# Prompt row sums of a product-key expert layer divided between TensorE and VectorE, with gelu values stored by token tile

## The chip, the cores and the metric

The kernel runs on one core of one Trainium2 chip. The metric is the device time of one execution in microseconds (us). Before the change three runs took 2674.08, 2677.42 and 2680.5 us; their median is 2677.42 us.

## The reference, cut to what matters

A two-layer trunk handles 384 tokens of width 1024: 128 prompt tokens (token tile 0) and 256 latent tokens (tiles 1 and 2). Each layer mixes the tokens (retention and mLSTM in layer 0, attention in layer 1) and then runs `_peer`, the part that is changed here. For each token and each of 8 heads, `_peer` picks 16 of 16384 experts, so 128 experts per token, with a softmax gate:

```
act = gelu(einsum("thkd,td->thk", u_tab[ib], xb)) * gb
out = einsum("thk,thkd->td", act, v_tab[ib])
```

`u_tab` and `v_tab` have 16384 rows of 1024 fp32 values (64 MB each per layer).

## The kernel before, in words

`peer_front` and `peer_experts` work through the 16384 experts as 128 **blocks** of 128. In the hidden stage (blocks 0 to 63 in `peer_front`, 64 to 127 in `peer_experts`), TensorE computes gelu inputs of one block for all 384 tokens; ScalarE applies gelu into `hidden_ring`, and the result goes to the DRAM tensor `hidden`. For the latent tokens VectorE multiplies the values of every expert by a gate (zero where an expert was not picked).

The **output stage** follows. Latent tokens are computed densely: for each of 128 blocks, `outs` makes 12 matmuls of 128x512 for the two latent tiles from `v_hi`, `v_lo` (the block of `peer_v` split into two fp32r parts) and `act_hi`, `act_lo` (the gated gelu values, split likewise). For each block ScalarE makes `v_hi` (L2164), and VectorE makes `v_lo` (L2300), `act_hi` (L2309) and `act_lo` (L2310). These parts have three buffers, so the parts of block o wait for TensorE to end block o-3. SyncE loads 2 MB of `peer_v` and 512 KB of gated values (`hidden_in`) for each four blocks, into two buffers each.

The 128 prompt tokens are not computed densely. Their 128 picked rows of `peer_v` are fetched by indirect DMA: one **row** DMA (L2212) brings the 128 rows of one token, 4 KB to each of 128 partitions, into one of `RING` = 11 slots. A **pick** DMA (L2220) brings the 128 gelu values of one token. Four tokens make one quad, 32 quads in all. `act_columns` (L2319, VectorE) multiplies the quad's gelu values by its gates into columns that are zero elsewhere, and `row_sums` (L2105, TensorE) multiplies those columns with the rows: eight 128x512 products per quad, which the profile shows as 16 instructions. `SET_AFTER` puts a set of two quads behind block 15 and every seventh block after that, 16 sets in all.

All engines work in program order. The places where they wait for each other in this stage:
- TensorE waits in `row_sums` for the columns (`acts_made`) and for the rows (`slot_in`).
- GpSimd issues row and pick DMAs in one fixed sequence. `row(j)` with j >= RING waits until the quad that used the slot is summed (`rows_summed`); everything behind it in the sequence waits too. The sequence starts when the last hidden values are in DRAM (`hg_out`), apart from `FREE` = 2 rows that are fetched earlier.
- VectorE waits for ScalarE's `v_hi`, for `hidden_in`, and in `act_columns` for the pick DMAs.

Behind the last block VectorE normalises tile 0 (whose sum is complete first), then tiles 1 and 2 (`norm_half`, L876 to L889), and writes the result.

## Time and profile before

| what | value |
|---|---|
| median of 3 runs | 2677.42 us |
| profiled execution: its own time | 2680.38 us |
| profiled execution: span | 2678.6 us |
| TensorE (PE) busy | 2604.6 us, 97% of the span |
| VectorE (DVE) busy | 1658.9 us, 62% |
| ScalarE (ACT) busy | 1022.3 us, 38% |
| GpSimd (POOL) busy | 720.7 us, 27% |
| output stage, layer 0, of which GpSimd issues | 990 to 1356 us |
| output stage, layer 1: first block to last row sums | 2256.44 to 2646.07 us |

The span runs from the first to the last instruction on the core; the profiled execution's own time is 1.8 us longer. Busy shares are averages over stages with different limits. Row sums, pick DMAs and row DMAs exist only in the two output stages, one per layer.

### The profile page before, as it was taken

To read this page: it belongs to the slowest core of one execution; us is meant where nothing else is said; L and a number is where in the kernel's file an instruction comes from. 1 tells how busy PE (TensorE), PEld (TensorE's weight loads), DVE (VectorE), ACT (ScalarE), POOL (GpSimd) and SP (SyncE) were. 2 spreads that over 40 slices of the span, in tenths; PEclk is the share of its full clock that TensorE was granted. 3 is DMA by queue.
4 is the path that set the end of the run, shared out by engine and by line. 5 is a ranking of instruction groups with operands and counts; after the bars stand their busy time and mean duration, and the time that the engine had idled before them with its cause. 6 is when DMAs were issued, how large, how long until landed. Compare 5 with 4: busy or idle time off the path is not lost. (4 is left out here: it accounts for less than half of the span.)

```text
span 2678.6 us, 39466 instructions
## 1 busy us (share of the span) xinstructions
PE 2604.6 (97%) x15833; PEld 2307.6 (86%) x15833; DVE 1658.9 (62%) x3306; ACT 1022.3 (38%) x1531; POOL 720.7 (27%) x688
## 2 busy tenths in 40 slices
PE   7998999999999999999999889999999999999998
PEld 6997789999999997777779679999999999777775
DVE  3447687879344456555576569987934445655556
ACT  3444433345433333333352554334543333333333
POOL 1001020000111117777723003000011111777773
PEclk9998899999999999999999989999999999999999
DMA  9653486547798869999964124344779886999995
GB/s 307 219 170 139 148 300 215 165 189 287 262 360 317 315 217 388 391 383 382 386 254 127 64 97 137 119 147 188 287 266 365 313 312 217 391 389 390 393 385 202
DMA packets 233941, 708.88 MB, mean 265 GB/s; under 512 B 22432, under 2 KB 154912, under 8 KB 211488
## 3 DMA queue, kind: packets, MB, share of 16 engines
q1 hardware_dynamic: 172912, 516.86, 52.7%
q0 software_dynamic: 60032, 189.01, 19.2%
q8 instruction: 127, 2.08, 0.3%
q10 hardware_dynamic: 816, 0.48, 0.1%
q14 instruction: 54, 0.44, 0.0%
HBM read 602.31 MB, written 103.98 MB: 264 GB/s over the span
## 5 line engine op out<-in xcount | busy, mean ns | idle before, releaser
L1410 PE MATMUL hidden_ps<-h_hi,u_hi 128*128 128x384 f32 x2016 | 680.3, 337 | 4.1 <-issue 3.1
L1410 PE MATMUL hidden_ps<-h_hi,u_lo 128*128 128x384 f32 x2016 | 674.0, 334 | 0.0
L1410 PE MATMUL hidden_ps<-h_lo,u_hi 128*128 128x384 f32 x2016 | 674.0, 334 | 0.0
L2300 DVE TENSOR_TENSOR v_lo<-v_slot,v_hi 128x1024 fp32r<-128x1024 f32 x248 | 303.9, 1225 | 269.2 <-ACT v_hi L2164 269.2
L2164 ACT ACTIVATE v_hi<-v_slot 128x1024 fp32r<-128x1024 f32 x248 | 263.0, 1060 | 515.0 <-PE out_ps L2093 503.0
L2093 PE MATMUL out_ps<-v_hi,act_hi 128*128 128x512 f32 x992 | 389.7, 393 | 0.0
L2093 PE MATMUL out_ps<-v_lo,act_hi 128*128 128x512 f32 x992 | 386.3, 389 | 0.0
L2093 PE MATMUL out_ps<-v_hi,act_lo 128*128 128x512 f32 x992 | 385.9, 389 | 0.0
L1410 PEld LDWEIGHTS hidden_ps<-h_hi,u_hi 128*128 128x128 f32 x2016 | 378.6, 188 | 6.9 <-issue 6.8
L1410 PEld LDWEIGHTS hidden_ps<-h_lo,u_hi 128*128 128x128 f32 x2016 | 378.7, 188 | 0.0
L1410 PEld LDWEIGHTS hidden_ps<-h_hi,u_lo 128*128 128x128 f32 x2016 | 378.5, 188 | 0.0
L2282 DVE TENSOR_TENSOR u_lo<-u_slot,u_hi 128x1024 fp32r<-128x1024 f32 x124 | 151.9, 1225 | 289.0 <-ACT u_hi L2149 289.0
L2220 POOL DMA_INDIRECT first_act<-hidden,hidden_number x256 | 272.9, 1066 | 154.1 <-issue 77.4
L2212 POOL DMA_INDIRECT row_slot<-in_peer_v,row_number x256 | 262.9, 1027 | 123.9 <-issue 67.7
L2093 PEld LDWEIGHTS out_ps<-v_hi,act_hi 128*128 128x128 f32 x992 | 186.1, 188 | 65.1 <-DVE act_lo L2310 16.4
L1764 DVE TENSOR_TENSOR u_lo<-u_slot,u_hi 128x1024 fp32r<-128x1024 f32 x132 | 164.2, 1244 | 119.2 <-ACT u_hi L1685 116.3
L2093 PEld LDWEIGHTS out_ps<-v_hi,act_lo 128*128 128x128 f32 x992 | 186.2, 188 | 39.0
L2093 PEld LDWEIGHTS out_ps<-v_lo,act_hi 128*128 128x128 f32 x992 | 186.2, 188 | 37.4
L1692 ACT ACTIVATE hidden_ring<-hidden_ps 128x384 f32<-128x384 f32 x128 | 63.0, 492 | 357.9 <-PE hidden_ps L1410 353.0
L2156 ACT ACTIVATE hidden_ring<-hidden_ps 128x384 f32<-128x384 f32 x128 | 63.0, 492 | 347.5 <-PE hidden_ps L1410 341.4
L2229 POOL MEMSET act_columns<- 128x1008 f32 x2 | 1.9, 945 | 569.5 <-POOLq L1422 569.5
L1685 ACT ACTIVATE u_hi<-u_slot 128x1024 fp32r<-128x1024 f32 x128 | 134.7, 1053 | 0.0
(502 smaller groups left out, 3968.9 us busy)
## 6 DMA issues: line engine op xcount, KB each, us to landing
u_slot<-in_peer_u SPq DMA_DIRECT2D x64, 2048.0 KB, 9.1
v_slot<-in_peer_v SPq DMA_DIRECT2D x64, 2048.0 KB, 9.9
hidden<-hidden_ring SPq DMA_DIRECT2D x64, 768.0 KB, 5.8
spread_gates<-spread SPq DMA_DIRECT2D x16, 2048.0 KB, 7.2
hidden_in<-hidden SPq DMA_DIRECT2D x64, 512.0 KB
ada_w_ring<-in_ada_w SPq DMA_DIRECT2D x48, 512.0 KB, 6.1
even_w_ring<-in_even_w SPq DMA_DIRECT2D x16, 1024.0 KB, 7.5
ada_w_ring<-in_ada_w SPq DMA_DIRECT2D x16, 1024.0 KB, 6.1
```

The lines of the kernel that those rows point to most:

```text
L1410: mm = pe.matmul(PH_[:, b, 0:T], u[:, b, k * P:(k + 1) * P], x[:, k, :], start=(k == 0 and part == 0), stop=(k == KB - 1 and part == 2))
L1685: act.activation(UH[:, n % 2, :], U[n // JC % 2][:, n % JC, :], ACT.Copy).then_inc(uh, 1)
L1692: act.activation(HG[:, m % 2, j, :], PH_[:, n % 2, 0:T], ACT.Gelu_apprx_tanh).then_inc(g_done, 1)
L1764: dve.tensor_tensor(UL[:, n % 2, :], U[n // JC % 2][:, n % JC, :], UH[:, n % 2, :].bitcast(F32), ALU.subtract).then_inc(ul, 1)
L2093: mm = pe.matmul(PO[:, t, c, :], a[:, at], x[:, c * CH:(c + 1) * CH], start=(o == 0 and part == 0), stop=(o == N_KEYS - 1 and part == 2), ...
L2156: act.activation(HG[:, m % 2, j, :], PH_[:, n % 2, 0:T], ACT.Gelu_apprx_tanh).then_inc(g_done, 1)
L2164: act.activation(hi, V[o // JC % 2][:, o % JC, :], ACT.Copy).then_inc(vh, 1)
L2212: pool.indirect_dma_start(ROWS[j % RING], None, table, bass.IndirectOffsetOnAxis(ap=IDXV[:, t:t + 1], axis=0)).then_inc(slot_in[j % RING], 16)
L2220: pool.indirect_dma_start(ACT0[:, t:t + 1], None, hidden, bass.IndirectOffsetOnAxis(ap=IDXG[:, t:t + 1], axis=0)).then_inc(pick_in[i % 8], 16)
L2229: pool.memset(SDW, 0.0).then_inc(zeroed, 1)
L2282: dve.tensor_tensor(UL[:, n % 2, :], U[n // JC % 2][:, n % JC, :], UH[:, n % 2, :].bitcast(F32), ALU.subtract).then_inc(ul, 1)
L2300: dve.tensor_tensor(lo, V[o // JC % 2][:, o % JC, :], hi.bitcast(F32), ALU.subtract).then_inc(vl, 1)
```

## The change

The prompt's 128 picks per token are halved. `HALF_PICKS` = 64.

- **TensorE's half.** One row DMA now brings 64 picks of two tokens (partitions 0 to 63 and 64 to 127), so that 64 row DMAs and 16 quads cover the 128 tokens. Each of the 16 places in `SET_AFTER` has one quad instead of two. The ring for these rows (`RING`) has 5 slots.
- **VectorE's half.** The other 64 picks of each token are fetched by 64 DMAs (`own_row`) that bring one picked row for each of the 128 tokens, a token to a partition. VectorE adds each to `row_sum`, weighted by a number per partition (`add_own_row`, one instruction of 128x1024). Four of them stand around each set, behind blocks -1, 0, +2 and +3 of it (`OWN_AFTER`). Their ring `OWN` has 6 slots, taken from the old ring of 11. At the end `row_sum` is added to tile 0's sum in PSUM, by two instructions of 128x512.
- **GpSimd's sequence** is rewritten: eight pick DMAs per quad instead of four, and the own rows between them. The count of indirect DMAs per layer stays at 256 (64 rows, 64 own rows, 128 picks).
- **act_hi** is made by ScalarE (`act_high`) instead of VectorE, ahead of `v_hi` of the same block.
- **gelu values by tile.** `hidden` and `hidden_ring` are laid out tile by tile, so that the two latent tiles of four blocks are 4 KB in one piece per partition instead of four pieces of 1 KB. VectorE's gating takes two instructions of half the size.
- In the front, the picks of tile 0 are transposed in paired form: one more VectorE copy, six more small ScalarE instructions, four more small VectorE instructions for the indices, once per layer.

```diff
-                RING, FREE = len(SLOT_AT), 2
+                RING, FREE = 5, 2
...
+                OWN = ROWS[RING:]
+                SUM0 = M.at("row_sum", 4096, [P, D])
...
-                QUADS = P // 4
-                SET = 2
-                SET_AFTER = [15 + 7 * i for i in range(16)]
+                QUADS = HALF_PICKS // 4
+                SET_AFTER = [15 + 7 * i for i in range(QUADS)]
+                OWN_AFTER = {SET_AFTER[j // 4] + (-1, 0, 2, 3)[j % 4]: j for j in range(HALF_PICKS)}
...
-                        sp.dma_start(HV[:, c % 2], HD[:, c, :, P:T]).then_inc(hg_in[c % 2], 16)
+                        sp.dma_start(HV[:, c % 2], HD[:, c, 1:TT]).then_inc(hg_in[c % 2], 16)
...
+                    def own_row(j):
+                        n, at = j % len(OWN), HALF_PICKS + j
+                        if j >= len(OWN):
+                            pool.wait_ge(own_added, j - len(OWN) + 1)
+                        pool.indirect_dma_start(OWN[n], None, table,
+                                                bass.IndirectOffsetOnAxis(ap=IDXV[:, at:at + 1], axis=0)).then_inc(own_in[n], 16)
...
+                    for j in range(len(OWN)):
+                        own_row(j)
                     picks(2)
                     picks(3)
-                    at = RING
                     for i in range(QUADS):
-                        while at < min(P, RING + 4 * i + 4):
-                            row(at)
-                            at += 1
+                        own = [j for j in range(len(OWN) + 4 * i, len(OWN) + 4 * i + 4) if j < HALF_PICKS]
+                        for j in own[:2]:
+                            own_row(j)
+                        for j in range(RING + 4 * i, min(HALF_PICKS, RING + 4 * i + 4)):
+                            row(j)
+                        for j in own[2:]:
+                            own_row(j)
                         if i + 4 < QUADS:
                             picks(i + 4)
...
-                        v.seq(dve.tensor_copy(hi, HV[:, c % 2, j, :]))
-                        dve.tensor_tensor(lo, HV[:, c % 2, j, :], hi.bitcast(F32), ALU.subtract).then_inc(a_done, 1)
+                        tiles = lambda x: x.rearrange("p (t k) -> p t k", t=2)
+                        dve.wait_ge(ah_ready, o + 1)
+                        dve.tensor_tensor(tiles(lo), HV[:, c % 2, :, j, :], tiles(hi.bitcast(F32)), ALU.subtract).then_inc(a_done, 1)
...
+                    def add_own_row(j):
+                        n, w = j % len(OWN), ACT0[:, HALF_PICKS + j:HALF_PICKS + j + 1]
+                        dve.wait_ge(acts_made, j // 4 + 1)
+                        dve.wait_ge(own_in[n], 16 * (j // len(OWN) + 1))
+                        if j == 0:
+                            dve.tensor_scalar(SUM0[:, :], OWN[n], w, None, ALU.mult).then_inc(own_added, 1)
+                        else:
+                            dve.wait_ge(own_added, j)
+                            dve.scalar_tensor_tensor(SUM0[:, :], OWN[n], w, SUM0[:, :], ALU.mult, ALU.add).then_inc(own_added, 1)
...
                             if t == 0:
                                 dve.wait_ge(rows_summed, QUADS)
+                                dve.wait_ge(own_added, HALF_PICKS)
+                                f = PO[:, 0, half, :]
+                                v.seq(dve.tensor_tensor(f, f, SUM0[:, half * CH:(half + 1) * CH], ALU.add))
```

The order of GpSimd's indirect DMAs at the start of the output stage of layer 0, before (`first_act` is a pick DMA, `row_slot` a row DMA; x8 means eight in a row):

```order
L2220 DMA first_act_1_3354<-hidden_1,hidden_number_1_3353 128x1 x8
L2212 DMA row_slot2_1_8139<-in_peer_v,row_number_1_3352 128x1024
...
L2212 DMA row_slot10_1_8147<-in_peer_v,row_number_1_3352 128x1024
L2220 DMA first_act_1_3354<-hidden_1,hidden_number_1_3353 128x1 x8
L2212 DMA row_slot0_1_8137<-in_peer_v,row_number_1_3352 128x1024
L2212 DMA row_slot1_1_8138<-in_peer_v,row_number_1_3352 128x1024
```

The same place in the changed kernel (L2256 are picks, L2242 TensorE's rows, L2249 VectorE's own rows):

```order
L2256 DMA first_act_1_3354<-hidden_1,hidden_number_1_3353 128x1 x16
L2242 DMA row_slot2_1_8151<-in_peer_v,row_number_1_3352 128x1024
...
L2249 DMA row_slot10_1_8159<-in_peer_v,row_number_1_3352 128x1024
L2256 DMA first_act_1_3354<-hidden_1,hidden_number_1_3353 128x1 x16
L2249 DMA row_slot5_1_8154<-in_peer_v,row_number_1_3352 128x1024
L2249 DMA row_slot6_1_8155<-in_peer_v,row_number_1_3352 128x1024
L2242 DMA row_slot0_1_8149<-in_peer_v,row_number_1_3352 128x1024
L2242 DMA row_slot1_1_8150<-in_peer_v,row_number_1_3352 128x1024
L2242 DMA row_slot2_1_8151<-in_peer_v,row_number_1_3352 128x1024
```

Before, 25 DMAs stood ahead of the first row that waits for a sum; now 43 do: 16 picks, 3 rows, 6 own rows, 16 picks and 2 own rows.

VectorE's order around the first set, before (`act_columns` is the set's two quads):

```order
L2300 TENSOR_TENSOR v_lo_1_8129<-v_slot1_1_8126,v_hi_1_8128 128x1024
L2319 TENSOR_TENSOR act_columns_1_8134<-first_act_1_3354,first_picks_1_3350 128x4 x2
L2309 CAST act_hi_1_8130<-hidden_in_1_8132 128x256
L2310 TENSOR_TENSOR act_lo_1_8131<-hidden_in_1_8132,act_hi_1_8130 128x256
L2300 TENSOR_TENSOR v_lo_1_8129<-v_slot1_1_8126,v_hi_1_8128 128x1024
```

and in the changed kernel:

```order
L2346 TENSOR_TENSOR v_lo_1_8141<-v_slot1_1_8138,v_hi_1_8140 128x1024
L2368 TENSOR_TENSOR act_columns_1_8146<-first_act_1_3354,first_picks_1_3350 64x4 x2
L2369 TENSOR_TENSOR first_act_1_3354<-first_act_1_3354,first_picks_1_3350 128x4
L2357 TENSOR_TENSOR act_lo_1_8143<-hidden_in_1_8144,act_hi_1_8142 128x256
L2346 TENSOR_TENSOR v_lo_1_8141<-v_slot1_1_8138,v_hi_1_8140 128x1024
L2376 TENSOR_SCALAR row_sum_1_8160<-row_slot5_1_8154,first_act_1_3354 128x1024
L2357 TENSOR_TENSOR act_lo_1_8143<-hidden_in_1_8144,act_hi_1_8142 128x256
L2346 TENSOR_TENSOR v_lo_1_8141<-v_slot0_1_3348,v_hi_1_8140 128x1024
L2379 SCALAR_TENSOR_TENSOR row_sum_1_8160<-row_slot6_1_8155,first_act_1_3354,row_sum_1_8160 128x1024
```

The copy into `act_hi` is gone from VectorE, and in four of each seven blocks a 128x1024 addition stands between `v_lo` of one block and `act_lo` of the next.

## Rows read from the trace of the kernel before

**Rows 1.** The page, part 1: engines, busy us, share of the span, instructions.

```profile
span 2678.6 us, 39466 instructions
PE 2604.6 (97%) x15833; PEld 2307.6 (86%) x15833; DVE 1658.9 (62%) x3306; ACT 1022.3 (38%) x1531; POOL 720.7 (27%) x688
```

**Rows 2.** Chain that ended last, layer 1: start us, us, engine and line.

```profile
2256.44 43.56 PE out_ps L2093 x192
2300.00 3.57 PE out_ps L2105 x32
2303.57 19.26 PE out_ps L2093 x84
...
2642.50 3.57 PE out_ps L2105 x32
2646.07 13.16 PE out_ps L2093 x57
```

**Rows 3.** Groups of instructions: shape, count | busy us, mean ns | idle before.

```profile
L2300 DVE TENSOR_TENSOR v_lo<-v_slot,v_hi 128x1024 fp32r<-128x1024 f32 x248 | 303.9, 1225 | 269.2 <-ACT v_hi L2164 269.2
L2310 DVE TENSOR_TENSOR act_lo<-hidden_in,act_hi 128x256 fp32r<-128x256 f32 x248 | 105.5, 425 | 8.6
L2309 DVE CAST act_hi<-hidden_in 128x256 fp32r<-128x256 f32 x248 | 71.6, 289 | 38.9 <-DMA hidden_in<-hidden 38.8
L877 DVE SCALAR_TENSOR_TENSOR X<-X,out_ps 128x512 f32<-128x512 f32 x10 | 6.9, 687 | 0.3
L2319 DVE TENSOR_TENSOR act_columns<-first_act,first_picks 128x4 f32<-128x4 f32 x64 | 7.6, 161 | 0.0
L2164 ACT ACTIVATE v_hi<-v_slot 128x1024 fp32r<-128x1024 f32 x248 | 263.0, 1060 | 515.0 <-PE out_ps L2093 503.0 <-issue 8.6 <-DMA v_slot<-in_peer_v 3.5
L2156 ACT ACTIVATE hidden_ring<-hidden_ps 128x384 f32<-128x384 f32 x128 | 63.0, 492 | 347.5 <-PE hidden_ps L1410 341.4 <-PEq L1422 6.1
```

**Rows 4.** Timeline of GpSimd, one set of layer 1: start us, us, instruction, idle before.

```profile
2461.99 1.01 POOL L2212 DMA_INDIRECT row_slot<-in_peer_v,row_number  x1 [1.70 <-PE out_ps L2105]
...
2482.02 1.10 POOL L2220 DMA_INDIRECT first_act<-hidden,hidden_number  x1 [0.30 <-issue]
2484.82 1.01 POOL L2212 DMA_INDIRECT row_slot<-in_peer_v,row_number  x1 [1.70 <-PE out_ps L2105]
```

**Rows 5.** Timeline of GpSimd, start of layer 1's output stage.

```profile
2262.28 1.00 POOL L2220 DMA_INDIRECT first_act<-hidden,hidden_number  x1 [38.35 <-DMA hidden<-hidden_ring]
...
2295.32 0.94 POOL L2220 DMA_INDIRECT first_act<-hidden,hidden_number  x1 [0.30 <-issue]
2302.16 1.63 POOL L2212 DMA_INDIRECT row_slot<-in_peer_v,row_number  x1 [5.89 <-PE out_ps L2105]
```

**Rows 6.** Timeline of GpSimd in 4 us of layer 1.

```profile
2447.00 0.95 POOL L2220 DMA_INDIRECT first_act<-hidden,hidden_number  x1 [0.31 <-issue]
2448.25 1.16 POOL L2220 DMA_INDIRECT first_act<-hidden,hidden_number  x1 [0.30 <-issue]
```

**Rows 7.** Timeline of VectorE in the same 4 us.

```profile
2447.36 1.23 DVE L2300 TENSOR_TENSOR v_lo<-v_slot,v_hi 128x1024 fp32r<-128x1024 f32 x1 [0.83 <-ACT v_hi L2164]
```

**Rows 8.** The row slots by tile, 2280 to 2650 us: time to landing.

```profile
DMA to landing us min/median/max: 4.7/9.1/14.7
```

**Rows 9.** Stretches: PE, PEld, DVE, ACT, POOL busy (count), PEclk, DMA share, GB/s.

```profile
2280.00:2290.00 10.00, 10.00 (x46) 8.29 (x45) 6.78 (x12) 4.03 (x4) 7.87 (x7) 1.00 1.05 414
2350.00:2400.00 50.00, 50.00 (x253) 36.83 (x252) 27.70 (x48) 15.91 (x15) 36.25 (x37) 1.00 1.02 387
2450.00:2500.00 50.00, 50.00 (x253) 36.84 (x252) 29.85 (x54) 15.96 (x16) 36.53 (x36) 1.00 1.03 400
```

**Rows 10.** Timeline of VectorE, end of layer 1: tile 0's normalisation, then tile 1's.

```profile
2652.63 0.69 DVE L876 TENSOR_TENSOR out_ps<-out_ps,GATE 128x512 f32<-128x512 f32 x1
2657.86 0.21 DVE L889 TENSOR_SCALAR ln_moments<-ln_moments 128x1 f32<-128x1 f32 x1
2659.33 0.70 DVE L876 TENSOR_TENSOR out_ps<-out_ps,GATE 128x512 f32<-128x512 f32 x1 [1.25 <-PE out_ps L2093]
```

More of the change, by code:

```diff
@@ L1870, in row_numbers @@
                         v.wait()
-                        v.mark(dve.scalar_tensor_tensor(IDXG[:, :], first, float(T), iota, ALU.mult, ALU.add))
+                        for s in range(2):
+                            r = slice(HALF_PICKS * s, HALF_PICKS * (s + 1))
+                            groups = lambda x: x[r, 0:HALF_PICKS].rearrange("p (g i) -> p g i", g=4)
+                            v.mark(dve.scalar_tensor_tensor(groups(second), groups(first), float(T),
+                                                            iota[r].rearrange("p (g h i) -> p g h i", g=4, h=2)[:, :, s, :], ALU.mult, ALU.add))
+                        v.mark(dve.tensor_scalar(second[:, HALF_PICKS:P], first[:, HALF_PICKS:P], float(T), CST[:, C_IDX:C_IDX + 1],
+                                                 ALU.mult, ALU.add))
                         v.mark(dve.scalar_tensor_tensor(ACT0[:, :], IDIG[:, :], -31.75, ACT0[:, :], ALU.mult, ALU.add))
                         v.wait()
+                        v.mark(dve.scalar_tensor_tensor(IDXG[:, :], IDIG[:, :], float(P - T), second, ALU.mult, ALU.add))
                         v.seq(dve.tensor_scalar(IDXV[:, :], ACT0[:, :], 4.0, float(l * N_KEYS * N_KEYS), ALU.mult, ALU.add))
@@ L1997, in peer_experts @@
                 slot_in = [sem(st, f"row_in{n}") for n in range(RING)]
+                own_in = [sem(st, f"own_row_in{n}") for n in range(len(OWN))]
+                own_added, ah_ready = sem(st, "own_row_added"), sem(st, "act_hi_ready")
                 pick_in = [sem(st, f"picked_in{n}") for n in range(8)]
@@ L2217, in picks @@
                             pool.wait_ge(acts_made, i - 7)
-                        for g in range(4):
-                            t = token(i, g)
-                            pool.indirect_dma_start(ACT0[:, t:t + 1], None, hidden,
-                                                    bass.IndirectOffsetOnAxis(ap=IDXG[:, t:t + 1], axis=0)).then_inc(pick_in[i % 8], 16)
+                        for at in [QUADS * g + i for g in range(4)] + [HALF_PICKS + 4 * i + g for g in range(4)]:
+                            pool.indirect_dma_start(ACT0[:, at:at + 1], None, hidden,
+                                                    bass.IndirectOffsetOnAxis(ap=IDXG[:, at:at + 1], axis=0)).then_inc(pick_in[i % 8], 16)
                     def early_load(e):
@@ L2287, in gate_chunk @@
                         dve.wait_ge(w_in[m % 2], 16 * (m // 2 + 1))
-                        a = each_key(HG[:, (FIRST_U + m) % 2, :, P:T])
-                        dve.tensor_tensor(a, a, each_group(W[m % 2]), ALU.mult).then_inc(gated, 1)
+                        for t in range(2):
+                            a = each_key(HG[:, (FIRST_U + m) % 2, 1 + t])
+                            ins = dve.tensor_tensor(a, a, each_group(of_tile(W[m % 2], t)), ALU.mult)
+                        ins.then_inc(gated, 1)
                     def gate_early(e):
@@ L2293, in gate_early @@
                         dve.wait_ge(early_w[e % 2], 16 * (e // 2 + 1))
-                        a = each_key(HV[:, e % 2])
-                        dve.tensor_tensor(a, a, each_group(WE[:, e % 2]), ALU.mult).then_inc(early_gated, 1)
+                        for t in range(2):
+                            a = each_key(HV[:, e % 2, t])
+                            ins = dve.tensor_tensor(a, a, each_group(of_tile(WE[:, e % 2], t)), ALU.mult)
+                        ins.then_inc(early_gated, 1)
                     def v_part(o):
@@ L2340, in _ @@
                         if o + 2 in SET_AFTER:
-                            for i in range(SET):
-                                act_columns(SET * SET_AFTER.index(o + 2) + i)
+                            act_columns(SET_AFTER.index(o + 2))
+                        if o in OWN_AFTER:
+                            add_own_row(OWN_AFTER[o])
                     if out is None:
@@ L2406, in peer @@
                 W0 = M.at("w_ring0", M.phase, [P, TD // TG, JC * TG])
[L2407 removed]
+                HD = nc.dram_tensor(unique("hidden"), [P, N_KEYS // JC, TT, JC, P], F32).ap()
                 PICK0 = M.at("first_picks", M.picks + 4096, [P, 3, P])
```

83 lines of the change are left out of this document (53 added, 30 removed).

## The prediction

> **What bounds the kernel now.** I read the page's first part, then the chain that ended last, and then each engine's timeline inside the stage that the change touches. The page shows TensorE busy for 97% of the span [rows 1]. The chain shows that the output stage of layer 1 is TensorE alone: seven blocks take 19.26 us, the row sums of a set 3.57 us, and the next set stands 22.83 us after the one before, sixteen times [rows 2]. Layer 0 has the same stage. The row sums are so 16 x 3.57 = 57.1 us of each layer. Nothing else is on the chain there, so a shorter set shortens the stage as long as nobody else needs the 22.83 us.
>
> Two others need nearly all of it. **GpSimd** starts a set's first row at 2461.99 and the next set's at 2484.82; of these 22.83 us it waited 1.70 for TensorE [rows 4]. Its 16 indirect DMAs take 21.13 us, 1.32 each. **The DMA engines** have a busy share of 1.02 to 1.03 at 387 to 400 GB/s [rows 9]. A set's traffic is 7/4 of 2 MB and of 0.5 MB and eight rows of 0.5 MB, 8.375 binary MB or 8.78 million bytes, and 8.78 in 22.83 us is 385 GB/s, as the rows show.
>
> GpSimd's price per issue depends on VectorE. An issue alone takes 0.95 us and 0.30 until the next [rows 6]. The issue at 2448.25 starts while VectorE's v_lo of 2447.36 still has 0.34 us to run [rows 7]; it takes 1.16 and ends 0.82 behind the end of v_lo. The one at 2447.00 began before v_lo did and took 0.95. So an issue that starts in a long VectorE instruction waits for it to end.
>
> **The change, per layer.**
>
> *Row sums.* One quad per set instead of two: 3.57 / 2 = 1.79 us less, 16 times: **-28.6 us**. TensorE alone would then need 19.26 + 1.79 = 21.05 us per set.
>
> *GpSimd's start.* GpSimd may begin only when the last hidden values are stored, at 2262.28; its 25 issues ahead of the first waiting row end with the one at 2295.32, so 34.3 us or 1.37 each [rows 5]. TensorE's ring of five holds one row of the second set. Rows 5 to 7, which the second set lacks, are now issues 44 to 46. Issue 46 starts at 2262.3 + 45 x 1.37 = 2324.0 and lands 9.1 us later (median; 4.7 to 14.7) [rows 8], at 2333.1. TensorE would be there at 2300.0 + 1.8 + 19.26 = 2321.1 [rows 2]. It waits **+12.0 us** (7.6 to 17.6 by the landings). Before, GpSimd stood idle for 5.89 us ahead of its first waiting row [rows 5]; now it comes to it late. The first own row is issue 20, starts at 2288.3 and lands at 2297.4, about when TensorE ends block 14 (2256.44 + 15 x 43.56 / 16 = 2297.3); the addition and act_lo behind it cost TensorE under 2 us, which the later wait of 12 swallows.
>
> *GpSimd's pace.* Behind the start it has 16 issues per set in 12 loops (then the picks run out), and it is late, so TensorE goes at GpSimd's pace where that is above 21.05. The trace has no own additions, so I bound it. If no issue met a VectorE instruction, 16 x 1.25 = 20.0 us: cost 0, as TensorE's 21.05 then rules. If each met one as the issue at 2448.25 did, 16 x 1.46 = 23.4: +28.2. I take today's 21.13 plus one more meeting of 0.21 (1.16 - 0.95) for each of the four additions, 22.0, since those are long instructions between SBUF operands as v_lo is, and GpSimd's issues already meet about one v_lo per block: 12 x 0.95 = **+11.4 us**. The Trainium skill ("SBUF — State Buffer", Who interferes with whom) says that a VectorE instruction with two SBUF inputs and a GpSimd instruction that reads SBUF shut each other out for a whole instruction, whichever starts first. By it the additions block as v_lo does, and the term stays; if they didn't, the pace would stay near 21.13 and the term near +1. The rows agree in one direction only: v_lo at 2447.36, which starts within an issue, takes its usual 1.23.
>
> *The end.* Tile 0's normalisation runs from 2652.63 to 2658.07, and tile 1's waits for TensorE until 2659.33 [rows 10]. Two PSUM additions (0.69 each, as L876) and the last two own additions (2.4) come ahead of it, and some eight casts of 0.29 go: 1.5 us more than now, against 1.3 of slack. With layer 0, where the next projection waits for tile 0, I take **+1.5** (0 to 4).
>
> *Costed at nothing.* VectorE: an addition is between v_lo's 1.225 and twice the 0.687 of the half-size form [rows 3], I take 1.22. Per set 7 x (1.225 + 0.425) + 4 x 1.22 + 3 x 0.16 = 16.9 of 21.05 us; before, 13.9 of 22.83. Its cover is the third buffer: a block's parts may be begun when block o-3 ends, two blocks or 5.5 us ahead. act_hi on ScalarE (under the 0.49 of 384 columns, say 0.4), v_hi 1.06, v_lo 1.225, an addition 1.22 and act_lo 0.425 make 4.3. Were that cover gone, each of the 64 additions could cost TensorE its 1.22, 78 us a layer. ScalarE has 7 x 1.46 = 10.2 of 21.05. gelu by tile and the halved gating add small overheads in the hidden stages, where VectorE waits for ScalarE; the larger pieces of hidden_in can only help a load for which VectorE idled 38.8 us [rows 3] and TensorE did not. The front's dozen small instructions stand beside TensorE's blocks.
>
> **Sum:** -28.6 + 12.0 + 11.4 + 1.5 = -3.7 per layer, -7.4 for both. The profiled execution took 2680.4, so 2673.0; it stands 3.0 above the median of the runs, so **2670.0 us**. With a pace of 21.5 to 22.4 this case spans 2658 to 2680.
>
> **Rivals.**
>
> *A: GpSimd holds the pace.* The casts that leave VectorE take 7 x 0.29 = 2.0 us of possible meetings away, and the issues may fall between the additions. At 21.05 or less the third term is 0: -15.1 per layer, -30.2, **2647 us**. For it: 20.0 is possible. Against: VectorE goes from 13.9 of 22.83 to 16.9 of 21.05 us.
>
> *B: the additions shut GpSimd out, and it is slower.* In an own block v_lo, addition and act_lo stand back to back, 2.87 us of a block's 19.26 / 7 = 2.75 us, and an issue finds VectorE occupied nearly always. At 23.4 us a set the third term is 28.2: +13.1 per layer, +26, **2704 us**. The point from which it decides: the second and fourth term leave 28.6 - 13.5 = 15.1 us, or 1.26 a set, so a pace above 22.3. For it: [rows 6, 7]. Against: in three of seven blocks no addition stands, and while TensorE waits for rows, VectorE soon waits too and lets GpSimd through.
>
> *C: the transfers bound.* At 21.05 us a set's 8.78 million bytes need 417 GB/s. The trace's 10 us with rows and weights together reached 414, its long stretches 387 and 400 [rows 9]. At their mean of 394 a set takes 22.3 us: 12 x 1.25 = 15.0 in place of 11.4, no change per layer (-0.1), **2677 us**. For it: shares above 1. Against: these stretches moved what TensorE's 22.83 us asked for, so they bound the engines from below only, and one-piece hidden loads may be cheaper. The Trainium skill ("DMA: Bandwidth & Descriptors", Specifications) puts HBM at about 358 GB/s per core, which would make 24.5 us a set and a slower kernel, 2730 by an estimate from that figure; the 387 to 400 GB/s measured here are above it, so it gets no chance of its own.
>
> That the halving isn't real can be excluded: 128 row-sum products per layer stand in the changed order, 256 before.
>
> **How the numbers follow.** Main case 0.38, A 0.25, B 0.20, C 0.17. A measurement of this kernel tells apart about 0.2%, 5.4 us (the three runs lie within 6.4). Faster by more than that is below 2672: A, two thirds of the main case, and 0.03 of C: 0.53. Within it, 2672 to 2683: 0.11 of the main case, 0.10 of C and 0.01 of B: 0.22. Slower: 0.25. The range reaches from 2643, a little below A, where a landing of 7 us would put it, to 2692, B at a pace of 22.9: +28.2 becomes 22.2, +7.1 a layer. Outside lie about 0.06 below and 0.13 above.
>
> **What would show it.** Right: sets of 16 row-sum instructions of 1.79 us; in layer 1 a gap of about 12 us ahead of the second set, with TensorE idle for a row DMA; sets 21.5 to 22.4 us apart up to the twelfth, GpSimd without waits in them, its mean issue above the 1.02 us (1.32 - 0.30) of today; from the fourteenth set 21.05. Wrong: no gap at the second set (the start is mis-sized); sets 21.05 apart with GpSimd waiting (A); GpSimd's issues at 1.16 throughout (B); transfers that land later than now while GpSimd waits (C); TensorE idle for v_lo or act_lo in the blocks with additions (VectorE's cover gone), or VectorE idle for own rows.

## The result, and the profile after

The changed kernel takes 2690.54 us (median of 11 runs, 2682.25 to 2698.86) where the kernel before takes 2677.42 (11 runs, 2674.07 to 2680.5): a ratio of **1.0055** with a 95% interval of 1.0043 to 1.0067; by the medians it is 13 us slower. The range held it; the forecast of 2670.0, faster, was wrong. The profiled execution took 2689.56 us, its span 2687.8, 9.2 more than before.

The page, part 1, as in [rows 1]:

```profile
span 2687.8 us, 38969 instructions
PE 2557.4 (95%) x15321; PEld 2289.7 (85%) x15321; DVE 1751.1 (65%) x3286; ACT 1101.7 (41%) x1799; POOL 722.2 (27%) x688
```

TensorE is busy for 47 us less and the kernel is still longer: TensorE now waits. The chain that ended last, layer 1 (start us, us, what), answers to [rows 2]:

```profile
2325.42 1.22 POOL row_slot L2242
2326.95 12.81 DMA row_slot<-in_peer_v,row_number
2339.90 3.64 PE out_ps L2122 x16
2343.53 3.82 PE out_ps L2112 x12
...
2457.84 18.19 DMA row_slot<-in_peer_v,row_number
2476.17 1.92 PE out_ps L2122 x16
2478.09 19.28 PE out_ps L2112 x84
2497.37 1.85 PE out_ps L2122 x16
```

Before, this chain was TensorE alone. Now GpSimd and row DMAs stand in it: at the second set a row lands 12.81 us after its issue, at another set 18.19. Between such places TensorE runs as predicted, 1.9 us of row sums and 19.28 of seven blocks.

GpSimd's timeline (start us, us, instruction, idle before): its first issue, its 25th, and row 7, the 46th, as in [rows 5]:

```profile
2263.26 1.00 POOL L2256 DMA_INDIRECT first_act<-hidden,hidden_number  x1 [38.56 <-DMA hidden<-hidden_ring]
...
2296.55 0.94 POOL L2249 DMA_INDIRECT row_slot<-in_peer_v,row_number  x1 [0.30 <-issue]
...
2326.95 0.94 POOL L2242 DMA_INDIRECT row_slot<-in_peer_v,row_number  x1 [0.30 <-issue]
```

Row slots by tile, 2280 to 2650 us, as in [rows 8], with landings now 13.1 in the median:

```profile
DMA to landing us min/median/max: 4.0/13.1/22.7
```

Stretches (PE, PEld, DVE, ACT, POOL busy, granted clock, DMA share, GB/s), as in [rows 9]:

```profile
2320.00:2340.00 20.00, 5.93 (x30) 4.64 (x32) 8.96 (x11) 4.10 (x6) 15.43 (x16) 0.71 0.86 323
...
2400.00:2600.00 200.00, 194.20 (x910) 147.28 (x909) 146.53 (x192) 87.32 (x128) 152.05 (x142) 0.99 1.02 402
```

In the long stretch the DMA engines are as full as before (1.02), and move 402 GB/s. In the stretch ahead of the second set they are not (0.86), TensorE is busy for 5.93 of 20 us, and its granted clock is 0.71.

From TensorE's timeline I worked out where a layer's output stage goes: from its first product to the first set, from there to the second, from the second to the sixteenth, and from the sixteenth to the last product. The lower rows are runs of the next section.

| us, layer 0 / layer 1 | to first set | to second | to sixteenth | to last product |
|---|---|---|---|---|
| before | 44.0 / 43.6 | 22.8 / 22.8 | 319.7 / 319.7 | 23.6 / 22.5 |
| after | 45.8 / 47.4 | 34.0 / 35.3 | 310.5 / 309.1 | 27.0 / 20.8 |
| e1, fewer picks ahead | 45.7 / 47.2 | 30.4 / 25.7 | 313.5 / 310.9 | 27.0 / 20.8 |
| e7, rows first as well | 46.5 / 45.7 | 25.9 / 21.2 | 309.2 / 311.2 | 26.5 / 20.8 |
| e12, rows first alone | 46.7 / 46.4 | 32.6 / 33.5 | 313.6 / 309.5 | 27.0 / 20.8 |
| e3, short additions | 45.5 / 45.9 | 33.8 / 34.7 | 307.2 / 309.5 | 25.6 / 20.8 |
| e5, narrow own rows | 45.9 / 47.8 | 32.2 / 31.8 | 302.2 / 300.4 | 26.9 / 20.8 |
| e6, half the picks | 43.7 / 43.7 | 21.2 / 21.2 | 300.4 / 303.8 | 25.3 / 20.8 |

The stage is 7.2 us longer in layer 0. In layer 1 the span ends 8.3 later against the first product. The 9.2 of the span is less than their sum, since between the stages 6.9 us come back (855.1 after, 861.9 before), while layer 0's first product comes 0.7 later. From 1400 to 1600 us the granted clock was 0.97 after and 0.93 before. In the runs below the stretch between the stages took 854 to 862 us, so I don't put it down to the change.

The time from the second set to the sixteenth is not one even pace. In layer 1 eight of its fourteen steps take 21.1 to 21.3 us, TensorE's own time, and the other six 21.9 to 25.9: five of those hold a wait for a row (8.3 us in all), and the first, 23.7, holds none; in it TensorE runs at a granted clock of 0.89 behind the long wait. Where a pace of 22.1 or 22.2 is named below, it is the mean of these steps.

### The profile page after: what moved, and what is told of

Its sections match the earlier page's. It is cut to its first block and busy times, and to the rows that moved or that the text cites. A ratio compares the mean times of both kernels' runs of the same rounds, so it can differ in the third digit from the quotient of the medians.

```text
span 2687.8 us, 38969 instructions
## 1 busy us (share of the span) xinstructions
PE 2557.4 (95%) x15321; PEld 2289.7 (85%) x15321; DVE 1751.1 (65%) x3286; ACT 1101.7 (41%) x1799; POOL 722.2 (27%) x688
## 3 DMA queue, kind: packets, MB, share of 16 engines
q0 software_dynamic: 60032, 189.01, 18.9%
## 5 line engine op out<-in xcount | busy, mean ns | idle before, releaser
L2346 DVE TENSOR_TENSOR v_lo<-v_slot,v_hi 128x1024 fp32r<-128x1024 f32 x248 | 303.8, 1225 | 228.6 <-ACT v_hi L2181 228.5
L2256 POOL DMA_INDIRECT first_act<-hidden,hidden_number x256 | 275.5, 1076 | 154.5 <-issue 77.4
L2190 ACT ACTIVATE act_hi<-hidden_in 128x256 fp32r<-128x256 f32 x248 | 103.4, 418 | 450.6 <-PE out_ps L2112 360.2
L2379 DVE SCALAR_TENSOR_TENSOR row_sum<-row_slot,first_act,row_sum 128x1024 f32<-128x1024 f32 x126 | 161.6, 1282 | 7.3 <-DMA row_slot<-in_peer_v,row_number 4.9
L2249 POOL DMA_INDIRECT row_slot<-in_peer_v,row_number x128 | 140.5, 1097 | 65.9 <-issue 33.5
```

The lines of the kernel that those rows point to most:

```text
L2190: act.activation(hi.rearrange("p (t k) -> p t k", t=2), HV[:, c % 2, :, j, :], ACT.Copy).then_inc(ah_ready, 1)
L2249: pool.indirect_dma_start(OWN[n], None, table, bass.IndirectOffsetOnAxis(ap=IDXV[:, at:at + 1], axis=0)).then_inc(own_in[n], 16)
L2256: pool.indirect_dma_start(ACT0[:, at:at + 1], None, hidden, bass.IndirectOffsetOnAxis(ap=IDXG[:, at:at + 1], axis=0)).then_inc(pick_in[i % ...
L2346: dve.tensor_tensor(lo, V[o // JC % 2][:, o % JC, :], hi.bitcast(F32), ALU.subtract).then_inc(vl, 1)
L2379: dve.scalar_tensor_tensor(SUM0[:, :], OWN[n], w, SUM0[:, :], ALU.mult, ALU.add).then_inc(own_added, 1)
```

## The experiments

Three groups: GpSimd's order at the start, the pace of the later sets, ScalarE. Each ratio is to the kernel before on the same chip.

### GpSimd's order at the start

**e1_fewer_picks_ahead**

```
                     picks(2)
-                    picks(3)
                     for i in range(QUADS):
...
-                        if i + 4 < QUADS:
-                            picks(i + 4)
+                        if i + 3 < QUADS:
+                            picks(i + 3)
```

> The changed kernel, but picks(3) no longer stand ahead of the loop and each turn of it asks for picks(i+3) instead of picks(i+4): rows 5 to 7, which the second set lacks, are then GpSimd's issues 36 to 38 and not 44 to 46. Theory S (the loss is the late start of the second set: 35.3 us between the first two sets of layer 1 where TensorE needs 21.1): the gap falls to 22 to 26 us, 9 to 13 us per layer, and the granted clock stays 1.00 around 2300 to 2350; the later sets keep their 22.1: 2668 to 2674 us. Rival G (GpSimd's 256 issues per layer are the bound, in whatever order): the second set comes earlier but the later ones lose it again, the last set of layer 1 stays within 3 us of where it is and the time stays at 2687 to 2693.

Measured: 2676.02 us, ratio 0.9998 (0.9984 to 1.0012): all of the loss is gone. The second set stands 25.7 us behind the first in layer 1 and 30.4 in layer 0. The sets behind it stand 22.3 us apart ((313.5 + 310.9) / 28), no less than after's 22.1. So theory S holds in direction: the time is 2 us above its range, the 30.4 outside its 22 to 26, and the granted clock over 2300 to 2350 us was 0.90 and not 1.00. G's time is excluded. The profiled execution, 2685.60, was the slowest of the twelve. GpSimd's order was worth some 14 us by the medians (2690.5 to 2676.0), although the issues are the same.

**e12_rows_first_only** and **e7_rows_first**: ahead of the wait for the hidden stores, GpSimd asks for what needs none.

```
+                    for j in range(FREE, RING):
+                        row(j)
+                    for j in range(len(OWN)):
+                        own_row(j)
                     for n in range(2):
                         pool.wait_ge(hg_out[n], 16 * (CHUNKS // 2))
                     for i in range(2):
                         picks(i)
-                    for j in range(FREE, RING):
-                        row(j)
-                    for j in range(len(OWN)):
-                        own_row(j)
```

> The changed kernel with rows 2 to 4 and own rows 0 to 5 ahead of the wait for the hidden stores, but picks(2) and picks(3) still ahead of the first waiting row and picks(i+4) in the loop: the one half of e7_rows_first, as e1_fewer_picks_ahead is the other. Theory S: the first set comes at 2291 to 2301, its own part of 3 to 4 us per layer and some 7 us of GpSimd's time are won, and the second set still stands 28 to 32 us behind it: 2674 to 2682 us. Rival: the first wait was all, 2666 to 2670 us as e7.

Measured: e12 takes 2688.53, ratio 1.0056 (1.0039 to 1.0073), as the change itself. The second set still stands 32.6 and 33.5 behind the first. My theory was 6 us too hopeful: the earlier start alone isn't worth anything that can be told.

> The changed kernel with another order at the start of GpSimd's part: rows 2 to 4 and own rows 0 to 5 are asked for ahead of the wait for the hidden stores (they need the row numbers only), then picks(0) and picks(1), then picks(2), and in the loop picks(i+3). Theories S and D: own row 0 is there long before block 14, the first set comes at 2300 to 2303, the second 21 to 24 us later, and from there the transfers' 22.1 us a set rule: last set of layer 1 at 2632 to 2638; 2660 to 2668 us, faster than both. Rival G (GpSimd's number of issues): as e1, 2672 to 2680 us. Rival M (the DMA engines only catch up later what was asked earlier): the later sets come at 22.6 or more, 2670 or more.

Measured: e7, which adds e1's edit, takes 2668.80, ratio **0.9972** (0.9963 to 0.9981), faster than both kernels. GpSimd's timeline in its layer 1 (its first row, then rows 5 to 7):

```profile
2247.63 1.77 POOL L2242 DMA_INDIRECT row_slot<-in_peer_v,row_number  x1 [34.79 <-DVE hidden_ring L2331]
...
2296.17 0.94 POOL L2242 DMA_INDIRECT row_slot<-in_peer_v,row_number  x1 [0.31 <-issue]
2297.41 0.94 POOL L2242 DMA_INDIRECT row_slot<-in_peer_v,row_number  x1 [0.30 <-issue]
2298.65 0.95 POOL L2242 DMA_INDIRECT row_slot<-in_peer_v,row_number  x1 [0.31 <-issue]
```

Row 7 is asked for 53.3 us behind TensorE's first product (2245.3), in the changed kernel 69.8 (2326.95 against 2257.2). The second set of layer 1 then stands 21.2 us behind the first: TensorE's own time. In layer 0 it stands 25.9 behind, with 4.6 us of waiting for a row. So most of the gap was the order. The halves are not alike: e1's is worth 14 us by itself, the rows first nothing by themselves and some 7 us beside it. The time is 0.8 us above the range of S and D. Rival M falls: the later sets did not pay for it (311.2 for fourteen, 22.2 each).

### The pace of the later sets

**e3_short_adds** (`SUM0[:, 0:8]` and `OWN[n][:, 0:8]` in the additions):

> The changed kernel, with VectorE's 64 additions per layer over 8 of 1024 columns only, so that the prompt rows lack most of VectorE's half; all DMAs, waits and orders as they are. It prices the 1.28 us of each addition. Rival V (the additions shut out GpSimd and hold up VectorE, and that is the loss): the issues fall back to 1.02 us mean, sets 2 to 16 come at 21.1 and the gap at the second set shrinks by 46 times 0.1: 2650 to 2660 us. Theories S and R: the additions matter for the pace only through some 0.1 us per issue and for the end of each layer, 3 us there and 2 to 6 us in the sets: 2676 to 2684 us, with the gap at the second set still above 31 us.

Measured: 2682.66 us, ratio 1.0027 (1.0016 to 1.0039). The groups of GpSimd's issues (count, busy us, mean ns, idle before), after and then e3:

```profile
L2256 POOL DMA_INDIRECT first_act<-hidden,hidden_number x256 | 275.5, 1076 | 154.5 <-issue 77.4 <-DMA hidden<-hidden_ring 77.1
L2249 POOL DMA_INDIRECT row_slot<-in_peer_v,row_number x128 | 140.5, 1097 | 65.9 <-issue 33.5 <-DVE row_sum L2379 32.3
L2242 POOL DMA_INDIRECT row_slot<-in_peer_v,row_number x128 | 135.2, 1056 | 51.6 <-issue 36.9 <-PE out_ps L2122 14.7
```

```profile
L2256 POOL DMA_INDIRECT first_act<-hidden,hidden_number x256 | 272.3, 1064 | 154.6 <-issue 77.4 <-DMA hidden<-hidden_ring 77.1
L2242 POOL DMA_INDIRECT row_slot<-in_peer_v,row_number x128 | 135.5, 1058 | 60.2 <-issue 36.9 <-PE out_ps L2122 23.3
L2249 POOL DMA_INDIRECT row_slot<-in_peer_v,row_number x128 | 132.1, 1032 | 62.7 <-issue 36.3 <-DVE row_sum L2379 26.4
```

Without the additions an own row's issue is 0.065 us shorter, a pick's 0.012, a row's no shorter: 4 x 0.065 + 8 x 0.012 = 0.36 us a set. Predicted were 4 x 0.21 = 0.84. The sets keep their pace (307.2 and 309.5 in place of 310.5 and 309.1). So V falls; the additions shut GpSimd out less than I took, and this doesn't set the pace. The kernel is still 8 us faster than the changed one, as S and R had it: in the profile 5.1 us in layer 0, of which 3.3 stand in the later sets and 1.3 at the end, and 2.1 in layer 1.

**e5_narrow_own_rows**

```
+                    narrow = table.rearrange("r (a d) -> (r a) d", d=64)
...
-                        pool.indirect_dma_start(OWN[n], None, table,
+                        pool.indirect_dma_start(OWN[n] if j < len(OWN) else OWN[n][:, 0:64], None, table if j < len(OWN) else narrow,
```

> The changed kernel, with VectorE's own rows from the seventh on read in 64 of 1024 columns only, so that most of VectorE's half of the prompt is not the model's: the same 256 indirect DMAs per layer, the same additions and waits, but 58 rows of 0.5 MB less to move, 6.9 in place of 8.8 million bytes a set. Theory D (the sets stand 22.1 us apart because the DMA engines are full: 8.78 million bytes at 400 to 405 GB/s are 21.7 to 22.0 us): rows land again in under 9 us and sets 3 to 16 come at TensorE's own 21.1 to 21.3; 2660 to 2668 us, with the gap at the second set still above 30. Rival G (GpSimd's issues set the 22.1): sets 2 to 16 stay at 21.9 to 22.3, 2684 to 2692 us.

Measured: 2672.10, ratio 0.9989 (0.9979 to 0.9998), 18 us below the changed kernel. Its stretch, the landing of its row slots, and its chain, from the seventh set of layer 1 on:

```profile
2400.00:2600.00 200.00, 198.41 (x937) 151.67 (x936) 149.94 (x196) 90.02 (x132) 149.10 (x144) 1.00 0.88 327
```

```profile
DMA to landing us min/median/max: 2.4/7.3/15.1
```

```profile
2440.29 1.92 PE out_ps L2122 x16
2442.21 19.28 PE out_ps L2112 x84
2461.49 1.85 PE out_ps L2122 x16
2463.35 19.31 PE out_ps L2112 x84
```

With the same instructions, but fewer bytes, row slots fill in 7.3 us in place of 13.1 (TensorE's rows alone, which are whole in both kernels: 7.3 in place of 13.0), and the chain is TensorE alone, 21.2 us a set. That is theory D's sign; its time was 4 us too low, because the gap at the second set and a few of 22.8 to 25.0 us behind it remained. G's unchanged pace is excluded, but not GpSimd's part in it, for its issues are shorter here too. From 2340 to 2580 us of layer 1, after and then e5:

```profile
L2256 POOL DMA_INDIRECT first_act<-hidden,hidden_number x86 | 91.7, 1067 | 26.2 <-issue 26.2
L2249 POOL DMA_INDIRECT row_slot<-in_peer_v,row_number x44 | 48.8, 1109 | 15.0 <-issue 11.6 <-DVE row_sum L2379 3.4
L2242 POOL DMA_INDIRECT row_slot<-in_peer_v,row_number x44 | 45.0, 1023 | 15.0 <-issue 12.8 <-PE out_ps L2122 2.2
```

```profile
L2257 POOL DMA_INDIRECT first_act<-hidden,hidden_number x88 | 92.4, 1050 | 26.8 <-issue 26.8
L2243 POOL DMA_INDIRECT row_slot<-in_peer_v,row_number x47 | 50.6, 1078 | 14.3 <-issue 14.3
L2250 POOL DMA_INDIRECT row_slot<-in_peer_v,row_number x44 | 42.9, 976 | 13.4 <-issue 13.1 <-DVE row_sum L2380 0.3
```

In these 240 us GpSimd waits 5.6 us for slots in the changed kernel and 0.3 in e5 (18.9 before); the rest are issues and the pauses between them. It makes 174 issues after and 179 in e5, so sixteen take 22.1 and 21.5 us, which are the paces of layer 1 in the two kernels (309.1 / 14 and 300.4 / 14). So GpSimd's list is nearly full in both, and e5 does not part the bytes from the issues.

**e6_half_picks** (only the four picks for TensorE's rows, and a wait for 64 in place of 128):

> The changed kernel without VectorE's four picks of each block, so that VectorE's rows are weighted by stale numbers: GpSimd has 12 indirect DMAs a set in place of 16 and 17 ahead of the first waiting row in place of 25, and the bytes are the same (a pick is 512 bytes). Theory D (transfers set the later sets, GpSimd's order the first two): the first set comes at 2300 to 2302, the second 21 to 25 us later, the others still 21.9 to 22.4 us apart: 2654 to 2664 us. Rival G (GpSimd's issues set the 22.1 too): all sets 21.1 to 21.3 apart, 2630 to 2642 us.

Measured: 2641.89, ratio 0.9875 (0.9860 to 0.9891). The start is as D had it, 43.7 and 21.2, so the late first set came from GpSimd's list too. But the later sets come 21.5 and 21.7 us apart, at full DMA engines:

```profile
2400.00:2600.00 200.00, 194.27 (x917) 146.10 (x919) 145.14 (x191) 87.21 (x128) 102.16 (x92) 0.99 1.01 406
```

The time is G's, at its upper end; the pace lies between the two, and D had not thought that GpSimd's spare time would do as much for it as fewer bytes. With time to spare GpSimd waits for slots (163 us over both layers) and asks for each row as soon as its slot is free, and a landing of 14.3 us (median, both layers) fits; the engines reach 406 to 411 GB/s. So the 402 GB/s of the changed kernel are what it moved and no ceiling, and nearly the same bytes go through in 21.5 to 21.7 us. Of the 1.0 us that the mean step of 22.1 stands above 21.1, 0.4 stay with twelve issues and 0.6 go. With the trace above I read it so: GpSimd's list, 16 issues of 1.08 + 0.30 = 22.1 us, holds the pace, and full DMA engines add the rest. What stays open: the packets of four picks are gone too, so e6 does not give the price of an issue alone.

**e2_ring7** (`RING, FREE = 7, 2`, which leaves VectorE four slots):

> The changed kernel with the eleven slots split seven to TensorE's ring and four to VectorE's, instead of five and six; every instruction else as it is. Theory R (a ring of five holds one row of the next set, so a set needs three rows that may be asked for only behind the set before: 1.9 for the set, 2.6 for two own rows, 3.9 for three rows and a landing of 13.1 are 21.5, and every late landing shows): with seven only one row is needed from behind, 1.9 + 2.6 + 1.3 + 13.1 = 18.9 under the 21.1 of TensorE; sets 2 to 16 fall from 22.1 to 21.2 to 21.5 us, 8 to 13 us per layer, the second set comes 2 to 4 us earlier: 2658 to 2672 us. Rival G (GpSimd's issue rate): nothing, 2687 to 2693. Rival V (VectorE's ring of four is now too short): VectorE waits for own rows and TensorE for VectorE, 2695 or more.

Measured: 2704.29, ratio 1.0117 (1.0101 to 1.0132): rival V. TensorE's waits in layer 1 (us in total, times, longest), first after, then e2:

```profile
PE out_ps L2122 <- DMA row_slot<-in_peer_v,row_number: 22.4, 6, 14.1
PE out_ps L2112 <- DVE act_lo L2357: 1.9, 1, 1.9
```

```profile
PE out_ps L2112 <- DVE act_lo L2357: 26.0, 8, 10.2
PE out_ps L2122 <- DMA row_slot<-in_peer_v,row_number: 0.6, 1, 0.6
```

Theory R was half right: with seven slots TensorE no longer waits for rows. But then VectorE waits for its own rows (42.0 us in 14 places, both layers, and 23.0 for the first of each layer), act_lo queues behind those additions, and TensorE waits for act_lo.

**e9_ring6** (e7's order, six and five slots) and **e10_rows_ahead** (e7's order, and in the loop `row(j)` ahead of all `own_row(j)`):

> The order of e7_rows_first with the slots split six and five: two rows of the next set are asked for behind the set before, not three. Theory D (full DMA engines and a ring that can't take a late landing set the later sets' 22.1 us together): TensorE's waits for rows fall from 13 us in layer 1 to 3 to 8 and the sets come 21.6 to 21.9 us apart; VectorE's five still suffice: 2658 to 2666 us. Rival V (VectorE's own rows come too late, as with four in e2_ring7): TensorE waits for act_lo instead, 2670 us or more.

> The order of e7_rows_first, and in the loop TensorE's four rows ahead of all four own rows: a row that TensorE waits for is asked for two issues, 2.6 us, earlier behind its set. Theory D with the ring of five: the late landings cost up to 2.6 us less each in some five sets per layer: 2658 to 2665 us. Rival G (GpSimd has no time to spare, and own rows that come later hold VectorE up): 2666 to 2674 us, no better than e7.

Measured: e9 2665.80, ratio 0.9973 (0.9959 to 0.9986), no different from e7; its time is in D's range, but its later sets are at 313.2 and 313.9, no faster, so a sixth slot alone doesn't bring the pace. e10 2683.59, ratio 1.0025 (1.0009 to 1.0040), 15 us worse than e7: VectorE waits 51.3 us for own rows in both layers. That is rival G's sign, and more than it gave. From 2340 to 2580 us GpSimd waits 1.2 us for slots and makes 168 issues, so sixteen take 22.9 us; the sets of layer 1 come 22.9 apart.

### The parts by themselves, and ScalarE

**e4_before_by_tile** (the kernel before, with the layout of gelu values alone):

> The kernel before, with the gelu values by tile alone: hidden ring, hidden values in DRAM, hidden_in and the pick numbers in that order, the gating in two halves; row sums and GpSimd's order as before. Theories S, R, V and G: no cost and no gain, 2674 to 2681 us, the output stages' sets at 22.8 as before. Rival L (the part by tile costs, by gelu's stores, by two gatings for one, or by the reads in larger pieces that take the DMA engines from the rows): 2683 us or more, the hidden stages longer or rows landing later than 9.1 us.

Measured: 2679.75, ratio 1.0011 (1.0001 to 1.0022): no cost that 0.2% can tell. Its sets stand 22.8 us apart.

**e8_act_hi_vector** (the changed kernel, with the cast back on VectorE):

> The changed kernel with act_hi made by VectorE again, as in the kernel before, instead of ScalarE. If the move to ScalarE is neutral (my theory: VectorE has the room while it waits for v_hi, ScalarE too): 2684 to 2694 us, sets as in the changed kernel. Rival V (VectorE has no room left: 16.9 us of work a set and 7 casts of 0.29 more are 18.9): TensorE waits for act_lo and v_lo in the blocks with additions, 2697 us or more. Rival H (act_hi stands ahead of v_hi on ScalarE and waits for hidden_in, so that a late load holds v_hi too): 2676 to 2684 us, with ScalarE's 38.7 us of waiting for hidden_in gone to VectorE.

Measured: 2718.30, ratio 1.0165 (1.0149 to 1.0181), 28 us worse than the changed kernel. My theory of a neutral move falls; V had the time, with another cause. TensorE waits for rows (29.5 us in layer 0), not for act_lo (2.3), and GpSimd's pick issues take 1.149 us in place of 1.076:

```profile
L2252 POOL DMA_INDIRECT first_act<-hidden,hidden_number x256 | 294.2, 1149 | 154.5 <-issue 77.4 <-DMA hidden<-hidden_ring 77.1
```

8 x 0.073 = 0.6 us a set. Fourteen sets of layer 0 take 322.0 in place of 310.5, 0.8 each, and of layer 1 314.6 in place of 309.1, 0.4 each. GpSimd has nothing left, so the casts show there.

**e11_before_act_hi_scalar** (the kernel before, with the cast on ScalarE ahead of `v_hi`):

> The kernel before, with act_hi made by ScalarE as in the changed kernel. TensorE has the buffers full there and VectorE 13.9 us of work in 22.8, so nobody waits for the cast: 2673 to 2680 us. Rival H (act_hi ahead of v_hi on ScalarE, behind a wait for hidden_in, costs by itself): 2683 us or more.

Measured: 2684.72, ratio 1.0037 (1.0023 to 1.0052): rival H. The stage grows by 3.2 and 3.1 us in the profile. ScalarE's cast, and VectorE's next v_lo, in its layer 1:

```profile
2282.95 0.42 ACT L2174 ACTIVATE act_hi<-hidden_in 128x256 fp32r<-128x256 f32 x1 [5.26 <-DMA hidden_in<-hidden]
2283.27 1.04 ACT L2165 ACTIVATE v_hi<-v_slot 128x1024 fp32r<-128x1024 f32 x1
```

```profile
2284.35 1.23 DVE L2314 TENSOR_TENSOR v_lo<-v_slot,v_hi 128x1024 fp32r<-128x1024 f32 x1 [5.07 <-ACT v_hi L2165]
```

A late hidden_in used to hold act_hi alone. Now v_hi stands behind that wait on ScalarE, and v_lo behind v_hi.

**e13_v_hi_first**, **e14_order_v_hi** (with e7's order), **e15_ring6_v_hi** (with e9's order and slots):

```
-                        act_high(o)
                         v_part(o)
+                        act_high(o)
```

> The changed kernel, with one pair of lines exchanged on ScalarE: v_hi of a block ahead of its act_hi, so that a late hidden_in holds act_hi only. Theory H (act_hi ahead of v_hi costs some 2 us at each first set and 2 to 4 us at each layer's end, since v_hi and v_lo queue behind a wait for hidden_in): from TensorE's first output product to the first set 44 to 46 us in place of 45.8 and 47.4, from the last set to the last product of layer 0 24 to 26 in place of 27.0; 3 to 6 us per layer, 2678 to 2685 us. Rival K (VectorE's own work and the own rows set both, the place of act_hi doesn't matter, as act_lo needs hidden_in anyway): 2686 to 2694 us.

> The order of e7_rows_first and v_hi ahead of act_hi on ScalarE. Theory H: 4 to 10 us below e7_rows_first, 2659 to 2665 us. Rival K: as e7, 2666 to 2672 us.

> The order of e7_rows_first, six slots for TensorE and five for VectorE, and v_hi ahead of act_hi on ScalarE. Theory H: 4 to 10 us below e9_ring6, 2656 to 2662 us. Rival K: as e9, 2663 to 2669 us.

Measured: e13 2685.98, ratio 1.0037 (1.0023 to 1.0051), whose interval overlaps that of the change. From the last set to the last product of layer 0 it takes 25.0 in place of 27.0, as H said; to the first set 45.8 and 48.4, no better, as K said. e14 2669.58 (0.9976, 0.9966 to 0.9986) is as e7: K. e15 takes **2660.95** (five runs; 0.9943, 0.9928 to 0.9958), the best of the kernels that leave nothing out, below e9 as H said. Why the exchange helps with six slots and not with five is open: e15's profiled run (2668.99, the slowest of the five) has stages of 406.9 and 399.7 us, not shorter than e7's 408.1 and 398.9 by what the medians say.

## Why the prediction was wrong

The sum was -28.6 + 12.0 + 11.4 + 1.5 = -3.7 per layer. In the trace it is, for layer 0 and layer 1, against the first product and 21.05 us a set:

| term | predicted | layer 0 | layer 1 | worked out |
|---|---|---|---|---|
| row sums | -28.6 | -28.6 | -28.6 | taken over |
| GpSimd's start | +12.0 | +14.8 | +18.1 | second set at 79.8 and 82.7, less (44.0, 43.6) + 21.05 |
| pace | +11.4 | +15.8 | +14.4 | 310.5 and 309.1, less 14 x 21.05 |
| the end | +1.5 | +5.2 | +4.4 | (27.0 - 23.6) and (38.8 - 36.2, last set to the span's end), plus 1.79, by which the last set is shorter |
| sum | -3.7 | +7.2 | +8.3 | |

**The step that failed is the size of the three costs:** GpSimd's start was put at +12.0 and measured 14.8 and 18.1, its pace at +11.4 and measured 15.8 and 14.4, the end at +1.5 and measured 5.2 and 4.4. All three were found, each in its place, and each was too small. The gain was eaten to 3.7 of 28.6 already in the forecast, so misses of 2 to 6 us each turned its sign.

- *Row sums*: nearly right. A set is 1.85 to 1.92 us, predicted 1.79, and seven blocks 19.28, so that TensorE alone needs 21.1 to 21.2 us and not 21.05. Over sixteen sets that is some 1.5 us a layer, which the table gives to the other terms.
- *GpSimd's start*: the mechanism was right, and e1 and e7 show it. I had issue 46 at 2324.0 and a landing of 9.1, the median of before [rows 8]. It came at 2326.95 (1.0 of that from a later start of the stage, the rest from issues 1.41 us apart in place of 1.37) and landed 12.8 later. Engines fuller than before don't explain this landing: from issue to landing their share was 0.98, at 380 GB/s, where [rows 9] has 1.02 to 1.05. The trace shows what was asked for at the same time: SyncE's loads, and the landing of the own row of 2321.45 and of rows 5 and 6, asked for at 2324.17 and 2325.42:

```profile
2323.08 0.33 SPq L2044 DMA_DIRECT2D v_slot<-in_peer_v  x1
2324.70 0.32 SPq L2067 DMA_DIRECT2D hidden_in<-hidden  x1
```

```profile
DMA to landing us min/median/max: 4.1/4.1/4.1
DMA to landing us min/median/max: 13.1/13.1/13.2
```

  The row ahead of the loads of 2 MB and 512 KB took 4.1 us, with the engines at a share of 0.19 from 2320 to 2323; those beside the loads took 13.1. No run moves the loads, so this cause is not shown; but a median over a stage was no price for this place. That TensorE's late first set is swallowed by this wait was right too: the second set is GpSimd's date.
- *GpSimd's pace*: the mean was nearly right (22.2 and 22.1 us a set, predicted 22.0, but over fourteen gaps instead of twelve), and GpSimd's list is nearly full, as forecast; the reason for its price was not. The forecast took 1.02 us for an issue of before from one set; over the whole kernel it is 1.05 (1.066 for picks, 1.027 for rows). Additions cost 0.36 us a set of issue time, not 0.84, and taking them away leaves the pace (e3). Rival C has a share: rows land in 13.1 us in place of 9.1, and with time to spare for GpSimd the pace stays at 21.5 and 21.7 (e6). With fewer bytes it is 21.6 and 21.5 (e5), but there the issues are shorter too. I had priced A, B and C as alternatives, where the two limits lie close together, and rival C over twelve sets, though the transfers go on when the picks have run out.
- *The end*: VectorE's two PSUM additions cost what was said (1.5 us), but they do not stand alone. VectorE's timeline, end of layer 1, as in [rows 10]:

```profile
2654.32 1.28 DVE L2379 SCALAR_TENSOR_TENSOR row_sum<-row_slot,first_act,row_sum 128x1024 f32<-128x1024 f32 x1
...
2659.92 0.41 DVE L2357 TENSOR_TENSOR act_lo_late<-hidden_in,act_hi_late 128x256 fp32r<-128x256 f32 x1
2660.26 0.69 DVE L2412 TENSOR_TENSOR out_ps<-out_ps,row_sum 128x512 f32<-128x512 f32 x1
...
2666.95 0.21 DVE L889 TENSOR_SCALAR ln_moments<-ln_moments 128x1 f32<-128x1 f32 x1
2667.20 0.70 DVE L876 TENSOR_TENSOR out_ps<-out_ps,GATE 128x512 f32<-128x512 f32 x1
```

  Tile 0 begins 11.3 us behind the last set (2649.0); before, 10.2 behind a set that was 1.7 longer. It takes 6.9 us in place of 5.4, and tile 1 follows without a wait: TensorE's slack of 1.25 is gone. Another 1.3 us stand behind VectorE's last instruction (6.6 us to the end of the span, 5.3 before); why stays open. With short own additions (e3) the span still ends 38.3 behind the last set, against 38.8: VectorE then waits for ScalarE's v_hi in their place (1.54 us ahead of the first late block), so most of this is not the own additions. ScalarE's order has part of it in layer 0 (e13: 2.0 us).
- *Costed at nothing*: by-tile layout right (e4). act_hi on ScalarE wrong both ways: in the kernel before it costs 3 us a layer (e11), and without it the changed kernel would be 28 us slower (e8); in the profiles, 22 us apart, 17 of them stand in the later sets, where GpSimd's picks take longer. The prediction had these casts in rival A, as 2.0 us of possible meetings, and not as what the change lives on.

Rival B's place was wrong: issues never came to 1.16 throughout (1.076, 1.097, 1.056). The Trainium skill ("SBUF — State Buffer", Who interferes with whom) has a VectorE instruction with two SBUF inputs and a GpSimd instruction that reads SBUF shut each other out for a whole instruction. What e3 shows of it is 0.065 us on an own row's issue for additions of 1.28. The Trainium skill ("DMA: Bandwidth & Descriptors", Specifications) puts HBM at about 358 GB/s per core. A rival by that figure was rightly left out: the engines moved 402 here, and 406 to 411 in e6.

## What to carry to other kernels

Before work is taken off the bound engine, write down the next two limits per period; where they lie within a few per cent (21.2 us for TensorE, 21.5 to 21.7 with full DMA engines in e6, 22.1 for GpSimd), the gain ends at the largest, and late arrivals add to it. In an order written by hand, count the issues ahead of the first request that someone waits for: here asking for eight picks less ahead, and for rows before a wait that they don't need, was worth 22 us with the same instructions in another order. Price a transfer for the place where it is asked for, not by the median of a stage: here the same 512 KB took 4.1 us or 13.1 within 4 us.

## What the runs showed of the hardware

TensorE's granted clock fell where it idled. In 2320 to 2340 us it was busy for 5.93 us at a granted 0.71, and behind a wait of 14.1 us the 16 row-sum instructions took 3.64 us in place of 1.90, and twelve products 3.82 in place of 2.75 (19.28 / 7): the lower of its two levels, 1.2 GHz, for a few us. That is 2.8 us of TensorE's time; but e7, whose clock stays 1.00 there, takes as long for the later sets, so no run shows that it cost the kernel anything, and none excludes it.

The landing time of TensorE's rows, 512 KB each, was 7.3 us in the median where the DMA engines had a share of 0.88 (e5), and 13.0 at 1.02 (after), with as many issues. The longest landing of a row slot in layer 1 was 22.7 us. TensorE's ring holds one row more than a set needs, and TensorE waited for rows in six places there, 22.4 us in all.

An indirect DMA of 128 rows or values took GpSimd about 1.07 us, with 0.30 to the next: 174 of them filled all but 5.6 of 240 us (after). Such a list is a limit of its own, beside the bytes that it moves.
